# Decayed attention on one core: two maps and 128 tokens to a unit of work, worked out one unit ahead

## The chip, the cores and the metric

The kernel runs on one core of one Trainium2 chip. The metric is the device time of one execution in microseconds (us). Of three runs the median is 2448.79, the lowest 2448.25 and the highest 2448.97.

## What is computed

A model of two blocks on 512 tokens of width 1024, all in fp32. The first block has four sublayers twice over (mixers, cross attention, MLP). The second has three attention branches in a row, each with its own input products, its own gate over the width of the model and its own product back to it; the three are summed and go through one last product. The change touches the attention of the third branch alone, the one with decay ("forgetting attention"): 8 heads of 64, each with a causal map of 512 by 512.

```python
def forgetting_attention(q, k, v, logf):      # q, k, v: 512 tokens x 8 heads x 64
    c = jnp.cumsum(logf, axis=1)
    ...
        s = jnp.einsum('bqhd,bkhd->bhqk', qblk, k).astype(jnp.float32) * scale
        decay = jnp.transpose(cblk, (0, 2, 1))[:, :, :, None] - c_k[:, :, None, :]
        s = jnp.where((dist >= 0)[None, None], s + decay, -jnp.inf)
        p = jax.nn.softmax(s, axis=-1)
        return jnp.einsum('bhqk,bkhd->bqhd', p.astype(v.dtype), v)
...
uc = jnp.einsum('bse,ed->bsd', yc * jax.nn.silu(gc), w_up_c[l])
gates = jax.nn.sigmoid(gm.reshape(B, S, N_BRANCH, D))
merged = gates[:, :, 0] * ua + gates[:, :, 1] * ub + gates[:, :, 2] * uc
```

## The kernel before

All matrices of weights are streamed: SyncE loads panels of 1 MB into `raw` (two slots), ScalarE (ACT) rounds each half of a panel to `w_hi` (L1294), VectorE (DVE) takes the rest as `w_lo` (L2087), and TensorE (PE) forms each product as three: hi by hi, hi by lo, lo by hi (`product3`, L588 to L590). One such triple with 512 columns is called a gate step below, where it belongs to the gates.

The third branch, "c", comes last. Its input products give `QK` (queries of two heads in one tile of 128 partitions: head 2j on partitions 0 to 63, head 2j+1 on 64 to 127; the keys likewise), `BV` (values) and `BG` (the silu of its gate). Then follows the stage that the change is about, `units("c", ...)`. In it PE has two kinds of work in one queue: the attention itself, in plain fp32, and 64 gate steps (`gate_products`), the product for the gate over the width of the model. These are spread over the units by `gate_steps`: 8 ahead of the first unit, the other 56 in even parts.

A unit is one head and one tile t of 128 tokens, 32 in all, t running from 0 to 3 within a head. The keys of tile t are (t + 1) x 128. The steps of a unit:
1. PE, `scores_c` (L1227): one product over 64 partitions, up to 512 columns.
2. DVE, `maxima`: adds the decay of the keys and of the rows on the way out of PSUM (L2752), the mask on the last 128 keys (L2756), and takes the maximum (L2757).
3. ACT, `exps` (L1975): exp in place, with the sum of each row.
4. PE, `turns_c` (L720 by the helper `turn`): t + 1 transposes into one bank; ACT copies them to `PT` (L2022).
5. PE, `values_c` (L1240): t + 1 products into 64 columns; DVE scales by the reciprocal sum (L2776) and by `BG` into `YT` (L2793).

Each fp32 product and each of its weight loads has two records in the trace; a transpose has one. Once a head, ahead of the turns of its t = 1, PE spreads the summed decay of the next head over all partitions (`key_sums`, four transposes by L720), and DVE brings it negated to SBUF (L2810).

The order on each engine is written out by hand. With `AHEAD` 2 the scores of the first two units come first; then for each unit: PE waits for its exp, turns it, issues the scores of the unit after next, then gate steps, waits for the copy, and forms the values. DVE: the reciprocal of the unit, the maxima of the unit after next, at times one split (L2087), the values, at times the key sums. ACT: the copy of the turns, the exps of the unit after next, at times the evacuation of a gate chunk (L2002) and a split (L1294).

PSUM has four banks for the gate products and four "aux" banks for the rest. The aux banks go round: `aux_plan` lists every use in the order of PE's instructions, use n gets bank n mod 4, and PE waits until use n - 4 has been read (`next_aux`). The same list tells DVE and ACT what to wait for.

The first branch, "a", has the same build with two maps to a unit (two maps share a head there), so 16 units, and works one unit ahead: PE issues the scores of the next unit (L1149, two products on the two halves of the partitions), some gate steps, turns (L720), gate steps, values (L1162). DVE forms the weighted difference of both maps (L2770) between exp and turns; PE waits for that. It has 12 gate steps for four units (the third branch: 14 for eight). The second branch works on pairs two units ahead.

Behind the units of "c" come four turns of `YT` (`turned_output`), the product back to the width of the model, and the last product `w_o` with the final norm.

Of the kernel before, what the change touches and what calls it, by code (L numbers as in the profile page):

```python
# [7 lines left out]
ALU = mybir.AluOpType  # L8
# [124 lines left out]
AHEAD = dict(a=1, b=2, c=2)  # L133

def aux_plan():

    e = [("x", k) for k in range(KC)] + [("par", i) for i in range(4)] + [("dt_rows",), ("dt",)]
    e += [("mem", j) for j in range(4)]

    def tile(c):  # L140
        return [("bc", c, q) for q in range(4)] + [("cb", c), ("xs", c, 0), ("xs", c, 1), ("bt", c)]

    e += [("acs",)] + tile(0)
    for c in range(TT):
# [41 lines left out]
    e += [("fc_rows",), ("fc",), ("cc",), ("cb_c", 0)]  # L186
    e += units("C", [(hd, t) for hd in range(8) for t in range(TT)], 1, 1, True) + [("Ct", j) for j in range(4)]
    return e
# [10 lines left out]
         + [("C", (hd, t)) for hd in range(8) for t in range(TT)])  # L199
# [40 lines left out]
def build(nc, w, out):  # L240

    with ExitStack() as ctx:
# [157 lines left out]
        def unit_row(b, u):  # L400
            return (EX[:, 0, 0, :], EX[:, 1, 0, :], EX[:, 0, 1, :] if b == "b" else NC)[unit_slot(b, u)]
# [162 lines left out]
        def _(pe):  # L564
# [539 lines left out]
            def units(b, us, scores, turns, values, before=lambda u: None):  # L1104
# [47 lines left out]
            def turns_a(u, dst):  # L1152
# [30 lines left out]
            def turns_b(u, dst):  # L1183
# [40 lines left out]
            def scores_c(u):  # L1224
                hd, t = u
                a = 64 * (hd % 2)
                pe.matmul(next_aux("C", "S", u, 0)[:, 0:(t + 1) * P], QK[a:a + 64, hd // 2, t * P:(t + 1) * P],  # L1227
                          QK[a:a + 64, 4 + hd // 2, 0:(t + 1) * P], start=True, stop=True).then_inc(aux_done, 1)

            def turns_c(u, dst):  # L1230
                row = unit_row("c", u)
                for kt in range(u[1] + 1):
                    ins = turn(dst[:, kt * P:(kt + 1) * P], row[:, kt * P:(kt + 1) * P])
                return ins

            def values_c(u, dst):
                hd, t = u
                e = UNIT[("C", u)] % 2
                for kt in range(t + 1):
                    ins = pe.matmul(dst[:, 0:64], PT[:, e, kt * P:(kt + 1) * P], BV[:, kt, hd * 64:(hd + 1) * 64],  # L1240
                                    start=(kt == 0), stop=(kt == t))
# [9 lines left out]
            def next_key_sums(u):  # L1251
                if u[1] == 1 and u[0] + 1 < 8:
                    key_sums(u[0] + 1)
# [3 lines left out]
            units("c", [(hd, t) for hd in range(8) for t in range(TT)], scores_c, turns_c, values_c, next_key_sums)  # L1257
# [7 lines left out]
        def _(act):  # L1265
# [653 lines left out]
            for n_, b in enumerate("abc"):  # L1919
# [35 lines left out]
                us = [(hd, t) for hd in range(8 if b == "c" else 4) for t in range(TT)]  # L1955
                B = b.upper()

                def exps(u):
# [3 lines left out]
                    if b == "a":  # L1962
# [3 lines left out]
                    elif b == "b":  # L1966
# [6 lines left out]
                    else:  # L1973
                        v = unit_row(b, u)[:, 0:(t + 1) * P]
                        ins = act.activation(v, v, ACT.Exp, bias=mxs[:, e, 0:1], accum_out=rs[:, e, 0:1])  # L1975
# [35 lines left out]
                for n, u in enumerate(us):  # L2011
# [4 lines left out]
                    if b == "b":  # L2016
# [5 lines left out]
                    free_aux(act.activation(dst, src, ACT.Copy), (B, "T", u, 0))  # L2022
# [46 lines left out]
        def _(dve):  # L2069
# [629 lines left out]
            for n_, b in enumerate("abc"):  # L2699
# [24 lines left out]
                def maxima(u):  # L2724
# [24 lines left out]
                    else:  # L2749
                        row = unit_row(b, u)  # L2750
                        bank = wait_aux(dve, ("C", "S", u, 0))
                        free_aux(dve.scalar_tensor_tensor(row[:, 0:n], EX[:, hd % 2, 1, 0:n],  # L2752
                                                          sm[:, 4 + t, hd:hd + 1], bank[:, 0:n], ALU.add, ALU.add),
                                 ("C", "S", u, 0))
                        aux_read(dve, "C", "S", u, 0)
                        step(dve.tensor_tensor(row[:, n - P:n], row[:, n - P:n], R[:, 0:P], ALU.add))  # L2756
                        ins = dve.tensor_reduce(mxs[:, e, 0:1], row[:, 0:n], AX.X, ALU.max, negate=True)  # L2757
                    ins.then_inc(S["unit_max"], 1)

                def weights(u):  # L2760
# [14 lines left out]
                    else:  # L2775
                        step(dve.reciprocal(rs[:, e, 2:3], rs[:, e, 0:1]))  # L2776

                def values(u, last):
# [12 lines left out]
                    else:  # L2791
                        s = slice(64 * hd, 64 * hd + 64)
                        ins = dve.scalar_tensor_tensor(YT[:, t, s], bank[:, 0:64], rs[:, e, 2:3], BG[:, t, s],  # L2793
                                                       ALU.mult, ALU.mult)
# [13 lines left out]
                def key_sums(hd):  # L2808
                    bank = wait_aux(dve, ("cb_c", hd))
                    free_aux(dve.tensor_scalar(EX[:, hd % 2, 1, :], bank[:, :], -1.0, None, ALU.mult), ("cb_c", hd))  # L2810
                    aux_read(dve, "cb_c", hd)

                us = [(hd, t) for hd in range(8 if b == "c" else 4) for t in range(TT)]
                split_chunks(2 * FIRST_PANEL[f"gm_{b}"] + W_SLOTS)
                if b == "c":
                    key_sums(0)
                for u in us[:AHEAD[b]]:
                    maxima(u)
                for n, u in enumerate(us):
                    weights(u)  # L2820
                    if n + AHEAD[b] < len(us):
                        maxima(us[n + AHEAD[b]])
                    if n:
# [4 lines left out]
                    if b == "c" and u[1] == 1 and u[0] + 1 < 8:  # L2828
                        key_sums(u[0] + 1)
# [86 lines left out]
```

## Time and profile before

The profiled execution took 2449.24 us; its span from first to last instruction is 2447.5 us.

| engine | busy us | share of the span |
|---|---|---|
| PE (matmul) | 2315.3 | 95% |
| DVE | 1304.6 | 53% |
| ACT | 921.1 | 38% |
| POOL | 154.9 | 6% |

The mean granted TensorE clock is 0.973 of full speed. The chain that ended last lies on PE for 83% of the span, on DVE for 10%, on ACT for 5%. How to read it: PE's products are pipelined, the durations of neighbours overlap, so the time that an instruction costs is the distance to the start of the next one. In the timeline equal neighbours are merged: "x8" are eight records, the second number is from the start of the first to the end of the last. A bracket at the end of a line is idle time of that engine ahead of it, and what ended it.

### The profile page before, as it was taken

The page shows a single profiled execution, that of the slowest core. Times are in us where ns is not written, and L with a number is a line of the kernel's source. Part 1 is how long each engine was busy: PE and PEld are TensorE (multiplying, and loading weights), DVE is VectorE, ACT ScalarE, POOL GpSimd, SP SyncE. Part 2 cuts the span into 40 slices and gives each one's busy share as a digit, 9 for nine tenths or more (in the row PEclk, how much of TensorE's full clock was granted, in tenths as well). Part 3 has the DMA queues.
Part 4 walks back from the last instruction along what each step waited for, and adds up shares of the span by engine and source line. Part 5 has one row for each costly group of instructions (what it writes and reads, how often), then busy time and mean ns, then how long its engine had stood idle before and what let it go on. Part 6 is the DMA issues. An engine that isn't in the chain of part 4 may idle for free.

```text
span 2447.5 us, 28890 instructions
## 1 busy us (share of the span) xinstructions
PE 2315.3 (95%) x11792; PEld 1915.0 (78%) x11792; DVE 1304.6 (53%) x1914; ACT 921.1 (38%) x1664; POOL 154.9 (6%) x115
## 2 busy tenths in 40 slices
PE   7999887998999999999899999999989899999998
PEld 6888676876888888888787678888869688779677
DVE  4998678644833334735554383343442833632564
ACT  3353662433423323334433232332333534623343
POOL 0000000040400000400004040000000000000000
PEclk9999889999999999999899999999989999999999
DMA  5332224332333232321142123332322132222112
GB/s 160 87 99 74 89 88 147 134 111 85 98 121 103 86 103 96 111 78 52 53 163 86 52 82 110 103 95 94 103 99 91 35 86 71 68 86 86 35 35 112
DMA packets 187193, 224.75 MB, mean 92 GB/s; under 512 B 16603, under 2 KB 153510, under 8 KB 186038
## 3 DMA queue, kind: packets, MB, share of 16 engines
q1 hardware_dynamic: 174800, 191.90, 24.9%
q10 hardware_dynamic: 11686, 22.62, 2.7%
q0 software_dynamic: 576, 8.39, 0.9%
q8 instruction: 94, 1.54, 0.3%
q14 instruction: 37, 0.30, 0.0%
HBM read 213.72 MB, written 9.18 MB: 91 GB/s over the span
## 4 chain that ended last, share of the span: by engine, by line
PE 83%; DVE 10%; ACT 5%; issue 2%; ACTq 1%; DVEq 0%
PE gemm L588 25%; PE gemm L589 24%; PE gemm L590 24%; PE aux L720 2%; DVE w_lo L2087 2%; PE aux L974 1%; PE aux L955 1%; PE aux L1227 1%; DVE x_lo L2110 1%; DVE work L2225 1%; ACT w_hi L1294 1%; DVE y_plain L2293 1%; PE aux L1240 1%; ACT work L1596 1%; PE aux L1197 0%
## 5 line engine op out<-in xcount | busy, mean ns | idle before, releaser
L2087 DVE TENSOR_TENSOR w_lo<-raw,w_hi 128x1024 fp32r<-128x1024 f32 x250 | 318.4, 1301 | 399.4 <-ACT w_hi L1294 398.7
L588 PE MATMUL gemm<-x_hi,w_hi 128*128 128x512 f32 x1288 | 517.0, 401 | 5.6 <-DVE w_lo L2087 3.2
L589 PE MATMUL gemm<-x_lo,w_hi 128*128 128x512 f32 x1288 | 505.1, 392 | 0.0
L590 PE MATMUL gemm<-x_hi,w_lo 128*128 128x512 f32 x1288 | 504.6, 392 | 0.0
L1294 ACT ACTIVATE w_hi<-raw 128x1024 fp32r<-128x1024 f32 x250 | 254.5, 1052 | 228.1 <-PE gemm L590 225.1
L588 PE MATMUL gemm<-w_hi,x_hi 128*128 128x256 f32 (+2 forms) x992 | 314.1, 317 | 5.7 <-DVE h L2174 5.4
L589 PE MATMUL gemm<-w_lo,x_hi 128*128 128x256 f32 (+2 forms) x992 | 309.4, 312 | 0.0
L590 PE MATMUL gemm<-w_hi,x_lo 128*128 128x256 f32 (+2 forms) x992 | 309.2, 312 | 0.0
L588 PEld LDWEIGHTS gemm<-x_hi,w_hi 128*128 128x128 f32 x1288 | 243.8, 189 | 81.5 <-issue 23.3
L590 PEld LDWEIGHTS gemm<-x_hi,w_lo 128*128 128x128 f32 x1288 | 243.7, 189 | 52.2
L588 PE MATMUL gemm<-w_hi,y_hi 128*128 128x512 f32 (+1 forms) x704 | 270.6, 384 | 10.6 <-DVE y_lo L2159 10.6
L589 PEld LDWEIGHTS gemm<-x_lo,w_hi 128*128 128x128 f32 x1288 | 243.8, 189 | 46.3
L589 PE MATMUL gemm<-w_lo,y_hi 128*128 128x512 f32 (+1 forms) x704 | 268.8, 382 | 0.0
L590 PE MATMUL gemm<-w_hi,y_lo 128*128 128x512 f32 x640 | 250.5, 391 | 0.0
L2083 DVE TENSOR_TENSOR w_lo<-raw,w_hi 128x1024 fp32r<-128x1024 f32 x112 | 134.7, 1221 | 160.0 <-ACT w_hi L1292 151.5
L588 PEld LDWEIGHTS gemm<-w_hi,x_hi 128*128 128x128 f32 x992 | 190.6, 192 | 22.0 <-DVE w_lo L2083 5.8
L589 PEld LDWEIGHTS gemm<-w_lo,x_hi 128*128 128x128 f32 x992 | 190.6, 192 | 10.9 <-issue 0.5
L590 PEld LDWEIGHTS gemm<-w_hi,x_lo 128*128 128x128 f32 x992 | 190.4, 192 | 10.2
L1292 ACT ACTIVATE w_hi<-raw 128x1024 fp32r<-128x1024 f32 x112 | 115.6, 1055 | 214.2 <-PE gemm L590 207.3
L588 PEld LDWEIGHTS gemm<-w_hi,y_hi 128*128 128x128 f32 x704 | 133.6, 190 | 38.2 <-issue 10.3
L589 PEld LDWEIGHTS gemm<-w_lo,y_hi 128*128 128x128 f32 x704 | 133.5, 190 | 25.8 <-issue 0.7
L2293 DVE SCALAR_TENSOR_TENSOR y_plain<-work,par,y_plain 128x512 f32<-128x512 f32 x217 | 149.1, 748 | 4.3 <-ACT y_plain L1498 3.9
(326 smaller groups left out, 2812.2 us busy)
## 6 DMA issues: line engine op xcount, KB each, us to landing
raw<-in_mlp_w_dram SPq DMA_DIRECT2D x64, 1024.0 KB, 5.4
raw<-in_w_in_dram SPq DMA_DIRECT2D x31, 1024.0 KB, 5.3
raw<-in_odd_w_in_dram SPq DMA_DIRECT2D x12, 1024.0 KB, 5.3
raw<-in_even_w_in_dram SPq DMA_DIRECT2D x10, 1024.0 KB, 5.3
raw<-in_even_w_in_dram SPq DMA_DIRECT2D x16, 512.0 KB, 5.5
raw<-in_xa_w_k_dram SPq DMA_DIRECT2D x8, 1024.0 KB, 5.4
raw<-in_xa_w_v_dram SPq DMA_DIRECT2D x8, 1024.0 KB, 5.2
raw<-in_even_w_out_dram SPq DMA_DIRECT2D x8, 1024.0 KB, 5.0
```

The lines of the kernel that those rows point to most:

```text
L588: pe.matmul(dst, a_hi, b_hi, start=first, stop=False)
L589: pe.matmul(dst, a_hi, b_lo, start=False, stop=False)
L590: return pe.matmul(dst, a_lo, b_hi, start=False, stop=last)
L720: return pe.transpose(dst, src, ident[0:src.shape[0], 0:src.shape[0]])
L955: ins = pe.matmul(dst[:, hh * MEM:(hh + 1) * MEM], XQ[:, k, t * P:(t + 1) * P], KT[:, k, :], start=(d == 0), stop=(d == 1))
L974: ins = pe.matmul(dst[:, :], VM[:, m, j * P:(j + 1) * P], PTX[:, m, j // 2, :], start=(m == 0), stop=(m == 1))
L1227: pe.matmul(next_aux("C", "S", u, 0)[:, 0:(t + 1) * P], QK[a:a + 64, hd // 2, t * P:(t + 1) * P], QK[a:a + 64, 4 + hd // 2, 0:(t + 1) * P] ...
L1292: act.activation(piece(w_hi, s), raw_piece(n, s % 2), ACT.Copy).then_inc(w_hi_ready, 1)
L1294: act.activation(w_hi[:, s % W_SLOTS, :, :], raw[:, n % RAW_SLOTS, :, (s % 2) * P:(s % 2 + 1) * P], ACT.Copy).then_inc(w_hi_ready, 1)
L2083: dve.tensor_tensor(piece(w_lo, s), raw_piece(s // 2, s % 2), piece(w_hi, s).bitcast(F32), ALU.subtract).then_inc(w_lo_ready, 1)
L2087: dve.tensor_tensor(w_lo[:, s % W_SLOTS, :, :], raw[:, s // 2 % RAW_SLOTS, :, half], w_hi[:, s % W_SLOTS, :, :].bitcast(F32), ALU.subtract)\
L2293: ins = dve.scalar_tensor_tensor(U[:, f, CONV_W - 1:] if last else acc, U[:, f, i:i + T], par_col("even_conv_w", i * KC + f), acc, ALU.mul ...
```

## The change

Two heads and one tile of 128 tokens make a unit of the third branch: 16 units (pair, t). Their scores are two products, one on each half of the partitions, into two aux banks; the turns go to two banks and are copied by two instructions; the values of both go to one bank. `EX` holds both maps of two units, as in the first branch; the key sums of four heads lie in `y_plain` (the memory of `y_lo`), and the copies of the turns of every second unit lie there too (`pair_weights`). The branch works one unit ahead instead of two. PE issues the scores of the next unit, half of the unit's gate steps, waits for exp, turns both maps, the other half, and the values. DVE takes the maxima of the next unit ahead of the reciprocals of this one. The key sums of heads 0 and 1 come first; those of the next pair come behind the values of t = 0 and t = 1.

```diff
-AHEAD = dict(a=1, b=2, c=2)
+AHEAD = dict(a=1, b=2, c=1)
@@ aux_plan
-            if name == "C" and u[1] == 1 and u[0] + 1 < 8:
-                out += [("cb_c", u[0] + 1)]
...
+            if name == "C" and u[1] < 2 and u[0] + 1 < 4:
+                out += [("cb_c", 2 * u[0] + 2 + u[1])]
...
-    e += units("C", [(hd, t) for hd in range(8) for t in range(TT)], 1, 1, True) + [("Ct", j) for j in range(4)]
+    e += units("C", [(pr, t) for pr in range(4) for t in range(TT)], 2, 2, True) + [("Ct", j) for j in range(4)]
@@ places
+        KEY_SUMS = y_plain[:, 2048:4096].rearrange("p (a b) -> p a b", b=T)
+
+        def pair_weights(u, g):
+            return PT[:, g, :] if UNIT[("C", u)] % 2 == 0 else y_plain[:, T * g:T * g + T]
@@ tensor, units
                 for n, u in enumerate(us):
-                    before(u)
-                    if b == "a":
+                    if b != "b":
                         if n + 1 < len(us):
                             scores(us[n + 1])
                         gate_products(b, (gate_steps(b, n - 1, len(us)) + gate_steps(b, n, len(us))) // 2)
+                    if b == "a":
                         pe.wait_ge(S["p_ready"], UNIT[(name, u)] + 1)
                     else:
                         pe.wait_ge(S["unit_exp"], UNIT[(name, u)] - 2 * TT + 1)
-                    turns(u, next_aux(name, "T", u, 0)).then_inc(aux_done, 1)
-                    if b != "a" and n + 2 < len(us):
+                    for g in range(2 if b == "c" else 1):
+                        turns(u, next_aux(name, "T", u, g), g).then_inc(aux_done, 1)
+                    if b == "b" and n + 2 < len(us):
                         scores(us[n + 2])
                     gate_products(b, gate_steps(b, n, len(us)))
-                    aux_read(pe, name, "T", u, 0)
+                    for g in range(2 if b == "c" else 1):
+                        aux_read(pe, name, "T", u, g)
                     values(u, next_aux(name, "PV", u)).then_inc(aux_done, 1)
+                    after(u)
@@ tensor, scores_c and values_c
+                pr, t = u
+                for g in range(2):
+                    a = 64 * g
+                    pe.matmul(next_aux("C", "S", u, g)[:, 0:(t + 1) * P], QK[a:a + 64, pr, t * P:(t + 1) * P],
+                              QK[a:a + 64, 4 + pr, 0:(t + 1) * P], start=True, stop=True).then_inc(aux_done, 1)
...
+                for g in range(2):
+                    s = slice((2 * pr + g) * 64, (2 * pr + g) * 64 + 64)
+                    for kt in range(t + 1):
+                        ins = pe.matmul(dst[:, 64 * g:64 * g + 64], pair_weights(u, g)[:, kt * P:(kt + 1) * P],
+                                        BV[:, kt, s], start=(kt == 0), stop=(kt == t))
...
             key_sums(0)
-            units("c", [(hd, t) for hd in range(8) for t in range(TT)], scores_c, turns_c, values_c, next_key_sums)
+            key_sums(1)
+            units("c", [(pr, t) for pr in range(4) for t in range(TT)], scores_c, turns_c, values_c, next_key_sums)
@@ scalar
+                    if b == "c":
+                        free_aux(act.activation(pair_weights(u, 0)[:, 0:(u[1] + 1) * P], bank[:, 0:(u[1] + 1) * P],
+                                                ACT.Copy), (B, "T", u, 0))
+                        bank = wait_aux(act, (B, "T", u, 1))
+                        src, dst = bank[:, 0:(u[1] + 1) * P], pair_weights(u, 1)[:, 0:(u[1] + 1) * P]
@@ vector, maxima
+                        for g in range(2):
+                            bank = wait_aux(dve, ("C", "S", u, g))
+                            free_aux(dve.scalar_tensor_tensor(EX[:, e, g, 0:n], KEY_SUMS[:, 2 * (hd % 2) + g, 0:n],
+                                                              sm[:, 4 + t, 2 * hd + g:2 * hd + g + 1], bank[:, 0:n],
+                                                              ALU.add, ALU.add), ("C", "S", u, g))
...
+                        step(dve.tensor_tensor(last, last, over(R[:, 0:P], 2), ALU.add))
+                        ins = dve.tensor_reduce(mxs[:, e, 0:2], EX[:, e, :, 0:n], AX.X, ALU.max, negate=True)
@@ vector, the loop over units
-                    weights(u)
+                    if b != "c":
+                        weights(u)
                     if n + AHEAD[b] < len(us):
                         maxima(us[n + AHEAD[b]])
+                    if b == "c":
+                        weights(u)
```

## Rows read from the trace of the kernel before

**Rows 1.** Busy time of each engine in the stage of the third branch
```profile
core 0: us, PE busy (x) PEld busy (x) DVE busy (x) ACT busy (x) POOL busy (x), PEclk, DMA share, GB/s
...
2253.00:2375.00 122.00, 111.63 (x549) 81.21 (x549) 70.14 (x182) 47.25 (x118) 0.00 (x0) 0.96 0.11 35
```

**Rows 2.** Waits of PE in that stage: us in total, times, longest
```profile
PE aux L720 <- DVE work L2810: 9.3, 7, 2.0
```

**Rows 3.** PE in order of time, one head of the stage (start, us, what)
```profile
2304.30 0.70 PE L1227 MATMUL aux<-work 64*128 64x256 f32 x2
2304.92 0.50 PE L588 MATMUL gemm<-x_hi,w_hi 128*128 128x512 f32 x1
...
2306.41 1.00 PE L1240 MATMUL aux<-work 128*128 128x64 f32 x8
2307.25 0.28 PE L720 MATMUL aux<-ident,work 128*128 128x128 f32 x1
2307.46 0.91 PE L1227 MATMUL aux<-work 64*128 64x384 f32 x2
2308.30 0.50 PE L588 MATMUL gemm<-x_hi,w_hi 128*128 128x512 f32 x1
2309.10 0.33 PE L1240 MATMUL aux<-work 128*128 128x64 f32 x2
2309.27 0.60 PE L720 MATMUL aux<-ident,sm 128*128 128x128 f32 x4
...
2310.02 1.12 PE L1227 MATMUL aux<-work 64*128 64x512 f32 x2
2311.07 0.50 PE L588 MATMUL gemm<-x_hi,w_hi 128*128 128x512 f32 x1
...
2312.57 0.56 PE L1240 MATMUL aux<-work 128*128 128x64 f32 x4
2314.19 0.52 PE L720 MATMUL aux<-ident,work 128*128 128x128 f32 x3 [1.07 <-DVE work L2810]
2314.64 0.49 PE L1227 MATMUL aux<-work 64*128 64x128 f32 x2
2315.05 0.50 PE L588 MATMUL gemm<-x_hi,w_hi 128*128 128x512 f32 x1
...
2316.55 0.78 PE L1240 MATMUL aux<-work 128*128 128x64 f32 x6
2317.16 0.61 PE L720 MATMUL aux<-ident,work 128*128 128x128 f32 x4
2317.70 0.70 PE L1227 MATMUL aux<-work 64*128 64x256 f32 x2
```

**Rows 4.** PE in order of time, a pair of scores in the first branch
```profile
1933.72 1.13 PE L1149 MATMUL aux<-work 64*128 64x512 f32 x4
...
1934.78 0.50 PE L588 MATMUL gemm<-x_hi,w_hi 128*128 128x512 f32 x1
```

**Rows 5.** Groups of equal shape in the third branch's stage: busy us, mean ns
```profile
L2793 DVE SCALAR_TENSOR_TENSOR work<-aux,rs,work 128x64 f32<-128x64 f32 x32 | 9.0, 281 | 17.2 <-PE aux L1240 16.6
...
L2752 DVE SCALAR_TENSOR_TENSOR work<-work,sm,aux 128x512 f32<-128x512 f32 x8 | 6.0, 747 | 6.9 <-PE aux L1227 6.9
...
L2022 ACT ACTIVATE work<-aux 128x512 f32<-128x512 f32 x8 | 4.8, 594 | 8.2 <-PE aux L720 8.2
```

**Rows 6.** DVE and ACT in order of time, a pair in the first branch
```profile
1937.05 1.22 DVE L2734 TENSOR_REDUCE mxs<-work 128x2 f32<-128x1024 f32 x1
...
1939.64 0.19 ACT L1965 ACTIVATION_READ_ACCUMULATOR work<-work,mxs 128x1 f32 x1
```

**Rows 7.** Windows of 4 us, PE alone; the third number group is the granted clock
```profile
2254.00:2258.00 4.00, 4.00 (x12) 0.50 0.18 25
...
2286.00:2290.00 4.00, 4.00 (x19) 0.70 0.80 259
2290.00:2294.00 4.00, 4.00 (x21) 0.88 0.00 0
```

**Rows 8.** Waits of PE in the units of the first branch
```profile
PE aux L720 <- DVE work L2770: 6.2, 6, 1.9
```

More of the change, by code:

```diff
@@ L198 @@
          + [("B", (hd, t)) for hd in range(4) for t in range(TT)]
-         + [("C", (hd, t)) for hd in range(8) for t in range(TT)])
+         + [("C", (pr, t)) for pr in range(4) for t in range(TT)])
 UNIT = {key: n for n, key in enumerate(UNITS)}
@@ L1102, in gate_products, with units @@
                     at["gate"] += 1
-            def units(b, us, scores, turns, values, before=lambda u: None):
+            def units(b, us, scores, turns, values, after=lambda u: None):
                 name = b.upper()
@@ L1224, in scores_c, with turns_c @@
             def scores_c(u):
[L1225 to L1231, printed above, removed]
+                pr, t = u
[3 more added lines that the diff above has]
+                              QK[a:a + 64, 4 + pr, 0:(t + 1) * P], start=True, stop=True).then_inc(aux_done, 1)
+            def turns_c(u, dst, g):
+                e = unit_slot("c", u)
                 for kt in range(u[1] + 1):
-                    ins = turn(dst[:, kt * P:(kt + 1) * P], row[:, kt * P:(kt + 1) * P])
+                    ins = turn(dst[:, kt * P:(kt + 1) * P], EX[:, e, g, kt * P:(kt + 1) * P])
                 return ins
             def values_c(u, dst):
[L1237 to L1241, printed above, removed]
+                pr, t = u
+                for g in range(2):
[3 more added lines that the diff above has]
+                                        BV[:, kt, s], start=(kt == 0), stop=(kt == t))
                 return ins
@@ L1251, in next_key_sums @@
             def next_key_sums(u):
-                if u[1] == 1 and u[0] + 1 < 8:
-                    key_sums(u[0] + 1)
+                if u[1] < 2 and u[0] + 1 < 4:
+                    key_sums(2 * u[0] + 2 + u[1])
             aux_read(pe, "cc")
             key_sums(0)
-            units("c", [(hd, t) for hd in range(8) for t in range(TT)], scores_c, turns_c, values_c, next_key_sums)
+            key_sums(1)
+            units("c", [(pr, t) for pr in range(4) for t in range(TT)], scores_c, turns_c, values_c, next_key_sums)
             turned_output("Ct", "c", 2)
@@ L1954, in _ @@
                 logs()
-                us = [(hd, t) for hd in range(8 if b == "c" else 4) for t in range(TT)]
+                us = [(hd, t) for hd in range(4) for t in range(TT)]
                 B = b.upper()
@@ L1961, in exps @@
                     act.wait_ge(S["unit_max"], UNIT[(B, u)] + 1)
[L1962 removed]
+                    if b != "b":
                         for m in range(2):
@@ L2021, in _ @@
                         src, dst = bank[:, 0:(u[1] + 1) * P], PT[:, e, 0:(u[1] + 1) * P]
-                    free_aux(act.activation(dst, src, ACT.Copy), (B, "T", u, 0))
+                    free_aux(act.activation(dst, src, ACT.Copy), (B, "T", u, 1 if b == "c" else 0))
                     if n + AHEAD[b] < len(us):
@@ L2749, in maxima @@
                     else:
[L2750 to L2754, printed above, removed]
+                        for g in range(2):
[3 more added lines that the diff above has]
+                                                              ALU.add, ALU.add), ("C", "S", u, g))
                         aux_read(dve, "C", "S", u, 0)
-                        step(dve.tensor_tensor(row[:, n - P:n], row[:, n - P:n], R[:, 0:P], ALU.add))
-                        ins = dve.tensor_reduce(mxs[:, e, 0:1], row[:, 0:n], AX.X, ALU.max, negate=True)
+                        aux_read(dve, "C", "S", u, 1)
+                        last = EX[:, e, :, n - P:n]
+                        step(dve.tensor_tensor(last, last, over(R[:, 0:P], 2), ALU.add))
+                        ins = dve.tensor_reduce(mxs[:, e, 0:2], EX[:, e, :, 0:n], AX.X, ALU.max, negate=True)
                     ins.then_inc(S["unit_max"], 1)
@@ L2775, in weights @@
                     else:
-                        step(dve.reciprocal(rs[:, e, 2:3], rs[:, e, 0:1]))
+                        step(dve.reciprocal(rs[:, e, 2:4], rs[:, e, 0:2]))
                 def values(u, last):
@@ L2791, in values @@
                     else:
-                        s = slice(64 * hd, 64 * hd + 64)
-                        ins = dve.scalar_tensor_tensor(YT[:, t, s], bank[:, 0:64], rs[:, e, 2:3], BG[:, t, s],
-                                                       ALU.mult, ALU.mult)
+                        for g in range(2):
+                            s = slice(128 * hd + 64 * g, 128 * hd + 64 * g + 64)
+                            ins = dve.scalar_tensor_tensor(YT[:, t, s], bank[:, 64 * g:64 * g + 64],
+                                                           rs[:, e, 2 + g:3 + g], BG[:, t, s], ALU.mult, ALU.mult)
                     free_aux(ins, (B, "PV", u))
@@ L2809, in key_sums @@
                     bank = wait_aux(dve, ("cb_c", hd))
-                    free_aux(dve.tensor_scalar(EX[:, hd % 2, 1, :], bank[:, :], -1.0, None, ALU.mult), ("cb_c", hd))
+                    free_aux(dve.tensor_scalar(KEY_SUMS[:, hd % 4, :], bank[:, :], -1.0, None, ALU.mult), ("cb_c", hd))
                     aux_read(dve, "cb_c", hd)
-                us = [(hd, t) for hd in range(8 if b == "c" else 4) for t in range(TT)]
+                us = [(hd, t) for hd in range(4) for t in range(TT)]
                 split_chunks(2 * FIRST_PANEL[f"gm_{b}"] + W_SLOTS)
@@ L2816, in _ @@
                     key_sums(0)
+                    key_sums(1)
                 for u in us[:AHEAD[b]]:
@@ L2827, in _ @@
                         gated(n - 1)
-                    if b == "c" and u[1] == 1 and u[0] + 1 < 8:
-                        key_sums(u[0] + 1)
+                    if b == "c" and u[1] < 2 and u[0] + 1 < 4:
+                        key_sums(2 * u[0] + 2 + u[1])
                 split_chunks(2 * FIRST_PANEL[f"gm_{b}"] + W_SLOTS + KC - 1)
```

15 lines of the change are left out of this document (6 added, 9 removed).

## The prediction

> **What bounds the kernel now.** I read the page first, then the busy time by stretches, then the waits of PE inside the stretch, and at last the instructions of that stretch in order of time. The stage of decayed attention is one stretch of 122 us, and PE is busy in 111.63 of it, DVE in 70.14, ACT in 47.25 [rows 1]. So PE carries it, and what can be won is of two kinds: PE's own instructions, and the holes in which it waits. The only large hole has one name: the turns of a unit (L720) wait for DVE's key sums (L2810), 9.3 us in 7 waits [rows 2]. Why: the aux banks are dealt out in turn, four of them, and the turns of unit t = 2 get the bank that the key sums of the next map took four places earlier; DVE empties that bank only after it has worked off the scores of unit t = 3.
>
> One map of a steady stretch shows all of it [rows 3]. Read the distances between starts, since the durations overlap. From the scores of t = 1 at 2304.30 to the same place one map later at 2317.70 are 13.40 us, two maps 26.80. In it:
> - scores: 0.62 (t = 1), 0.84, 1.05, 0.41, together 2.92; the length goes with the keys
> - a gate step (three products of 512 columns): 0.80 alone right behind scores (2308.30 to 2309.10), 1.49 for two (2304.92 to 2306.41): 0.69 each, and 0.11 once after scores
> - values: 0.84 for eight records (t = 3), 0.17 for two (t = 0), 0.61 for six, so 0.39 for four: 2.01 a map, 0.11 a record
> - key sums and the turns of t = 1: 0.75 for six transposes; the turns of t = 0, 2, 3 are 0.21, 0.45, 0.54. This is 0.11 for each transpose and 0.10 more before scores. Key sums are then 0.44
> - the wait: 1.62 from the values of t = 1 to the turns of t = 2, of which 0.39 are values: 1.23.
>
> **The change part by part.**
> Scores. Two maps of one unit are now issued one after the other on rows 0 to 63 and 64 to 127. The first branch does just this already, and there the pair of t = 3 takes from 1933.72 to 1934.78, 1.06 us [rows 4], where one map alone takes 1.05 [rows 3]. So a pair costs what one did: bounds are 1.06 (side by side) and 2.10 (one behind the other), and I take the lower, since it is the same shape, type and array half. Per two maps that removes 2.92 us.
> The 0.10 ahead of scores and the 0.11 behind them appear at every group of scores; of eight per two maps four go: 0.4 + 0.44 removed.
> The Trainium skill, "TensorEngine Tiling (Array Packing)", section "Key Properties", says that changing the tiling mode drains TensorE; the trace agrees in kind, by the 0.10 and 0.11 just read.
>
> Turns and values. The number of transposes and of products stays. Of the turns, 20 per two maps at 0.11 are 2.2, now behind gate steps and ahead of gate steps, so without the switch to half the array. Values: a pair is twice one, plus 0.05 as the records run on without a break: 4.22 per two maps.
> Key sums. Two per two maps, 0.88, now placed behind the values of t = 0 and t = 1.
> Gate steps: 56 over 16 units, 3.5 each, in the order 1 and 2 (t = 0, 2), 2 and 2 (t = 1, 3): ahead of the turns and behind them. Fourteen per two maps, 9.66.
> The new sum per two maps: 9.66 + 4 x 0.11 + 2.92 + 4 x 0.10 + 2.2 + 4.22 + 0.88 = 20.7 us, if PE never waits.
>
> The waits. The key-sum wait goes: key sums now take the bank that the second turns of the next unit get, and DVE empties it ahead of the maxima of the unit after next, with a pair of scores and the first gate steps in between. What is late next? With one unit ahead, the turns of t = 3 need exp of t = 3, whose scores were issued one unit earlier. From the end of the scores PE has: one gate step 0.80, turns of t = 2 0.66, two gate steps 1.38, values 1.27, the switch 0.10, scores of the next t = 0 0.41, two gate steps 1.49: 6.1 us. DVE and ACT need in that time: two sums at 0.75 [rows 5], the mask on 256 elements (not in this trace; between nothing and the 0.75 of 512 elements, I take 0.4), the maximum over 1024 elements 1.22, which ends at 1938.27, and the exp pair with its sums until 1939.83, 1.56 [rows 6]: 4.7. Slack 1.4. At the very last unit no scores follow, so 0.6 less: 0.8. Shorter t have less to do in the chain and about the same gate steps above it.
> ACT now has two copies behind the turns, 0.59 each [rows 5], and PE's values wait for the second. Two gate steps, 1.38, stand between; the first copy starts while the second map still turns (0.44), so the copies end some 0.8 us after the turns: hidden, slack 0.6. Behind the copies queue the exps of the next unit and the gate evacuation; they have the slack above. If this cover were gone, each unit would pay up to 0.8 us, 13 in all.
> On DVE the reciprocal now stands behind the maxima of the next unit and ahead of the split and the values. The turns do not use it, only the values do on their way out, so nothing on PE waits. DVE's work stays near 70 us, of a stage that would be some 97 long. Other edits cost nothing: the same bytes at other places (the low half of y is free in this stage, the last readers of it being the products ahead of it), and one more key sum before the first scores, counted below. No DMA is added; SP's loads of the next weights wait for DVE's splits, which go by PE's gate steps, so they move with PE.
>
> **The sum.** 26.8 - 20.7 = 6.1 per two maps, four times 24.4. Added: the waits were in truth 7, and longer at the first maps; 9.3 us plus 7 x 0.16 for the rest of each hole are 10.4, where eight times 1.23 are 9.8: 0.6 more. In the windows from 2286 to 2294 the granted clock fell to 0.70 and 0.88, behind a second long wait; 4 x 0.30 + 4 x 0.12 = 1.7 us lost there [rows 7], and with the waits gone I expect this back. Taken off: the second key sum at the stage's start, where the clock is at 0.50 (1.2 of 2.4 GHz) [rows 7], 0.9 of which I count 0.6; one more 0.28 [rows 5] of DVE before the last turns, and 0.2 for small holes. Result 24.4 + 0.6 + 1.7 - 0.6 - 0.3 - 0.2 = 25.6 us. The profiled execution took 2449.24 (span 2447.5), so 2423.6; it stands 0.45 above the median of the runs, so 2423.2.
>
> **The rivals.**
> First: the chain from scores over DVE and ACT to the turns comes bare, since one unit ahead is less than two. For it speaks the first branch, which works one ahead on pairs and waits 6.2 us in 6 waits for DVE [rows 8]. Against it: there DVE's weighted difference of both maps stands between exp and turns, and the maxima of the next unit stand behind that, so each lateness is handed on; here neither holds, and there are 14 gate steps where the first branch has 12. Its price is that of the first branch: 6.2, giving 2429.4.
> The Trainium skill, "TensorEngine Tiling (Array Packing)", section "PSUM Bottleneck", warns that tiling speeds up TensorE but not PSUM evacuation, and names this same outcome; the first branch's waits are what this trace has of it.
> Second: the pair does not run side by side in this stage. Then the scores cost 2.92 more per two maps: 11.7, giving 2434.9. What the first branch shows speaks against it [rows 4].
> Third, slower than before: the chain is bare in full. If ACT reaches the exps of a unit only when PE already stands at its turns, each unit pays the whole chain behind its scores, 4.7 at t = 3 and about half of that at t = 0, some 3.5 in the mean: 16 x 3.5 = 56 us lost against 25.6 won, giving 2479. It decides from 1.6 us of waiting per unit; with the slack of 1.4 it takes 3 us more in the chain than the rows give. ACT's queue is the place for it (copies, exps, gate evacuation and split in one line), and ACT is busy only 47.25 of 122 [rows 1].
> That the granted clock stays or falls low elsewhere costs about what it did, 1.7, and lies in the forecast's own range.
>
> **How the numbers follow.** Forecast 0.80, its own range 2421 to 2427 (0.6 to either side for the holes, 1.7 if the clock does not come back, up to 2 for copies that are not quite hidden). First rival 0.09, second 0.03, third 0.04, and 0.04 for a mixture that cancels the gain. The range 2420.5 to 2430.5 takes in the forecast and the first rival. What a measurement here can tell from no change is about 0.2%, 4.9 us; the forecast, the first and the second rival are all beyond it. Faster 0.93, same 0.03, slower 0.04.
>
> **What would show it.** The pair of scores of t = 3 at 1.05 to 1.1 us to the next gate product, in 16 groups; no wait of L720 for the key sums; a period of 20.7 us per two maps; the stage some 26 us shorter, and all behind it unchanged and that much earlier; a clock of 1.00 between the stage's start and its end. Wrong would be: waits of the turns for ACT's exp over 1 us per unit, values waiting for the second copy, or a period above 23.

## The result: 27 to 29 us faster, and what the changed kernel's profile shows

The changed kernel takes 2419.33 us (median of 4 runs, 2417.22 to 2421.02) where the kernel before took 2448.52 in the same comparison (2446.81 to 2448.97): a ratio of 0.9882 with a 95% interval from 0.9865 to 0.9899, 29.2 us. Later comparisons, on three chips, gave 0.9890 (0.9875 to 0.9905), 0.9888 (0.9873 to 0.9903) and 0.9888 (0.9871 to 0.9904). All 16 times of the changed kernel together have the median 2418.9 and reach from 2414.3 to 2421.0; 25 times of the kernel before have 2446.8, from 2443.2 to 2449.3. That is 27.9 us between the medians and 27.7 between the means. The forecast was 25.6 us and 2423.2; the time lies 1.2 us below the low end of the stated range, 2420.5.

The profiled execution of the changed kernel took 2417.22 us; its span is 2415.5. First the busy time of its third branch's stage, to be held against [rows 1] (same columns). Lines have moved: L588 to L590 are L594 to L596 now, L720 is L726, L1227 is L1237, L1240 is L1251, L2810 is L2827.

```profile
2247.00:2341.00 94.00, 93.02 (x540) 74.08 (x540) 60.50 (x131) 43.14 (x114) 0.00 (x0) 0.96 0.14 45
```

PE is busy in 93.02 of 94 us; it had holes of 10 us in [rows 1]. The waits of PE from 2250 to 2350 are these two and no others. The key sums' 9.3 us of [rows 2] are gone and nothing has come in their place:

```profile
PE aux L726 <- DVEq L2815: 0.7, 1, 0.7
PE gemm L594 <- DVE y_lo L2124: 0.3, 1, 0.3
```

Now one pair of heads in order of time, the counterpart of [rows 3] (start, us, what). It begins and ends at the scores of t = 1:

```profile
2278.53 0.70 PE L1237 MATMUL aux<-work 64*128 64x256 f32 x4
2279.16 0.50 PE L594 MATMUL gemm<-x_hi,w_hi 128*128 128x512 f32 x1
...
2279.96 0.38 PE L726 MATMUL aux<-ident,work 128*128 128x128 f32 x2
2280.10 0.48 PE L594 MATMUL gemm<-x_hi,w_hi 128*128 128x512 f32 x1
...
2281.57 0.55 PE L1251 MATMUL aux<-work 128*128 128x64 f32 x4
2281.96 0.60 PE L726 MATMUL aux<-ident,sm 128*128 128x128 f32 x4
2282.49 0.92 PE L1237 MATMUL aux<-work 64*128 64x384 f32 x4
2283.34 0.50 PE L594 MATMUL gemm<-x_hi,w_hi 128*128 128x512 f32 x1
...
2288.02 1.13 PE L1237 MATMUL aux<-work 64*128 64x512 f32 x4
2289.08 0.50 PE L594 MATMUL gemm<-x_hi,w_hi 128*128 128x512 f32 x1
...
2295.20 1.03 PE L726 MATMUL aux<-ident,work 128*128 128x128 f32 x8
2295.99 0.47 PE L594 MATMUL gemm<-x_hi,w_hi 128*128 128x512 f32 x1
...
2297.46 1.89 PE L1251 MATMUL aux<-work,y_plain 128*128 128x64 f32 x16
2299.28 0.70 PE L1237 MATMUL aux<-work 64*128 64x256 f32 x4
```

The scores are four records now, and yet as short as two were: 1.06 us at t = 3 (2288.02 to 2289.08), 0.85 at t = 2, 0.63 at t = 1, against 1.05, 0.84 and 0.62 for one map in [rows 3]. The period is 2299.28 - 2278.53 = 20.75 us; 20.7 was worked out, and 26.80 it was.

How near does the chain from scores over DVE and ACT come to the turns? This is the unit of t = 3 across the engines, from its scores to its turns:

```profile
2267.26 1.13 PE L1237 MATMUL aux<-work 64*128 64x512 f32 x4
2268.49 1.41 DVE L2766 SCALAR_TENSOR_TENSOR work<-y_plain,sm,aux 128x512 f32<-128x512 f32 x2 [0.43 <-PE aux L1237]
2270.00 0.42 DVE L2772 TENSOR_TENSOR work<-work 128x256 f32<-128x256 f32 x1
2270.46 1.22 DVE L2773 TENSOR_REDUCE mxs<-work 128x2 f32<-128x1024 f32 x1
2271.72 0.72 ACT L1977 ACTIVATE work<-work,mxs 128x512 f32<-128x512 f32 x1 [1.19 <-DVE mxs L2773]
...
2273.05 0.19 ACT L1977 ACTIVATION_READ_ACCUMULATOR work<-work,mxs 128x1 f32 x1
...
2274.45 1.04 PE L726 MATMUL aux<-ident,work 128*128 128x128 f32 x8
```

The scores are done at 2268.3, exp at 2273.24, the turns start at 2274.45: a chain of 4.9 us (4.7 forecast) and a slack of 1.2 (1.4 forecast). The mask on 256 elements, which no row of before showed, takes 0.42; the forecast took 0.4.

### The profile page after: what moved, and what is told of

The parts are those of the page before. It is cut to its first block, busy times and chain, and to the rows that moved or that the text cites. A ratio compares the mean times of both kernels' runs of the same rounds, so it can differ in the third digit from the quotient of the medians.

```text
span 2415.5 us, 28810 instructions
## 1 busy us (share of the span) xinstructions
PE 2293.1 (95%) x11792; PEld 1904.8 (79%) x11792; DVE 1296.4 (54%) x1866; ACT 919.0 (38%) x1664; POOL 155.0 (6%) x115
## 4 chain that ended last, share of the span: by engine, by line
PE 83%; DVE 10%; ACT 5%; issue 2%; ACTq 1%; DVEq 0%
PE gemm L594 25%; PE gemm L595 24%; PE gemm L596 24%; PE aux L726 2%; DVE w_lo L2101 2%; PE aux L980 1%; PE aux L961 1%; DVE x_lo L2124 1%; ACT w_hi L1306 1%; DVE work L2239 1%; PE aux L1251 1%; DVE y_plain L2307 1%; ACT work L1608 1%; PE aux L1237 1%; PE aux L1206 0%
## 5 line engine op out<-in xcount | busy, mean ns | idle before, releaser
L594 PE MATMUL gemm<-x_hi,w_hi 128*128 128x512 f32 x1288 | 515.8, 400 | 6.1 <-DVE w_lo L2101 3.7
L596 PE MATMUL gemm<-x_hi,w_lo 128*128 128x512 f32 x1288 | 504.2, 391 | 0.0
L594 PE MATMUL gemm<-w_hi,x_hi 128*128 128x256 f32 (+2 forms) x992 | 313.8, 316 | 5.7 <-DVE h L2188 5.4
L596 PE MATMUL gemm<-w_hi,x_lo 128*128 128x256 f32 (+2 forms) x992 | 309.1, 312 | 0.0
L594 PEld LDWEIGHTS gemm<-x_hi,w_hi 128*128 128x128 f32 x1288 | 243.4, 189 | 75.0 <-issue 17.1
L596 PEld LDWEIGHTS gemm<-x_hi,w_lo 128*128 128x128 f32 x1288 | 243.0, 189 | 51.9
L594 PE MATMUL gemm<-w_hi,y_hi 128*128 128x512 f32 (+1 forms) x704 | 271.5, 386 | 10.6 <-DVE y_lo L2173 10.6
L596 PE MATMUL gemm<-w_hi,y_lo 128*128 128x512 f32 x640 | 250.5, 391 | 0.0
L594 PEld LDWEIGHTS gemm<-w_hi,x_hi 128*128 128x128 f32 x992 | 190.2, 192 | 22.0 <-DVE w_lo L2097 5.8
L596 PEld LDWEIGHTS gemm<-w_hi,x_lo 128*128 128x128 f32 x992 | 190.1, 192 | 10.3
L594 PEld LDWEIGHTS gemm<-w_hi,y_hi 128*128 128x128 f32 x704 | 134.4, 191 | 38.2 <-issue 10.3
```

The lines of the kernel that those rows point to most:

```text
L594: pe.matmul(dst, a_hi, b_hi, start=first, stop=False)
L596: return pe.matmul(dst, a_lo, b_hi, start=False, stop=last)
```

## Where the other microseconds come from: the same code, executed again

From the first key sums (2248.00) to the last turns (2340.16) the stage takes 92.2 us. Before it took 118.7 (2253.49 to 2372.18). So the stage gave 26.5. But the profiled executions differ by 32.0 us (2449.24 and 2417.22), and the rest, 5.5 us, was already there when the stage began. These are the first instructions of the third branch's sums of decay, in code that is the same in both, in the two first profiles (the kernel before, the changed kernel):

```profile
2250.80 0.39 PE L1220 MATMUL aux<-sm,triu 128*128 128x8 f32 x2 [0.69 <-ACT work L1952]
```

```profile
2245.02 0.39 PE L1229 MATMUL aux<-sm,triu 128*128 128x8 f32 x2 [0.69 <-ACT work L1964]
```

5.8 us apart, ahead of every changed instruction. The same windows of both, PE alone (busy, granted clock, DMA), show what differs: the granted clock. First the kernel before, then the changed one.

```profile
200.00:360.00 160.00, 139.13 (x892) 0.89 0.26 88
...
1180.00:1370.00 190.00, 170.47 (x785) 0.92 0.27 92
```

```profile
200.00:360.00 160.00, 139.41 (x911) 0.91 0.26 88
...
1180.00:1370.00 190.00, 170.57 (x780) 0.93 0.27 92
```

0.02 of 160 us and 0.01 of 190 are 5 us. Is that the change, or chance? Two runs repeat the two kernels without an edit.

> The kernel before, unchanged, profiled once more. Question: the first profiles of before and after differ by 5.6 us in code that is the same in both, ahead of the third branch's units, at places where one of them shows a granted clock of about 0.5 for some 3 us and the other does not. If that is chance from execution to execution, this profile has its low-clock stretches at other places than the first of before, and the time up to the first key sums of the third branch moves by 1 to 5 us. If it belongs to the kernel, the stretches lie where they lay and that time agrees within 0.5 us. The stage itself, from the first key sums to the last turns: 118.7 us again, or 1.7 less if its second dip of the clock is absent.

Measured: one time, 2449.09 us, where seven plain runs of the same kernel on that chip had 2443.18 to 2448.28. The profile puts the sums of decay at 2250.61, the clock at 0.89 and 0.92 in the two windows, the stage at 118.7 with the same dip. It is a twin of the first profile, so this run alone speaks for the rival.

> The changed kernel, unchanged, timed again. Stage theory: the change is worth its stage, 26.3 us by the first pair of profiles (25.6 were forecast), and the rest of the measured 29.2 is chance of the clock elsewhere; then the difference here lies between 24 and 29 and the stage is 92.6 us again within 0.5. Rival: the change also helps the code ahead of it (another layout of the program); then this profile too is some 5 us ahead of both of before when the third branch's stage begins, and the difference is 29 or more.

Measured: 2419.13 us (2417.68 to 2420.45), where before had 2445.96: 26.8 us. The sums of decay stand at 2245.47, the stage takes 92.2. The difference is within the 24 to 29 of the stage theory; the profile is again 5 us early, as the rival had it.

The clock records of all the profiles tell what the 5 us are made of, but not what decides them. Added up from the start to the first sums of decay, the time at half clock is 119.5 us in both profiles of the kernel before; 109.2 in three and 112.6 in one of the four of the changed kernel; 105.8 in the kernel of the next section, which is the kernel before with one small edit in the third branch (its sums of decay stand at 2244.59, earlier than any); and 116.1, 116.1 and 102.4 in the next three kernels, which are small edits of the changed one. Half of such time is lost. Take that half from the place of the sums of decay, and 2190.4 to 2191.7 is left in ten of the thirteen profiles (2192.3 to 2194.8 in the other three). So nearly all of the 5 us is time at half clock, in code that is the same. It does not go with the change as such, since a small edit of either kernel moves it by 3 to 7 us. That it is pure chance is not shown either: the profiles of one and the same kernel agree within 0.2 us (before) and 1.9 us (changed) at the sums of decay. What the plain times show is that 5 us are not gained for good: the profiled executions of the kernel before, 2449.24 and 2449.09 us, lie above 24 of its 25 plain times. What makes an execution take more or less of its time at half clock there was not found.

## Experiments on the parts

**The key sums' bank.** The kernel before, single maps, two ahead, with nothing changed but the place of the key sums:

```diff
@@ aux_plan, units
-            if name == "C" and u[1] == 1 and u[0] + 1 < 8:
-                out += [("cb_c", u[0] + 1)]
             turns = [(name, "T", u, j) for j in range(nt)]
...
             if pv:
                 out += [(name, "PV", u)]
+            if name == "C" and u[1] == 1 and u[0] + 1 < 8:
+                out += [("cb_c", u[0] + 1)]
@@ tensor, units
                 for n, u in enumerate(us):
-                    before(u)
...
                     values(u, next_aux(name, "PV", u)).then_inc(aux_done, 1)
+                    before(u)
```

> The kernel before with one part of the change: the key sums of the next head are issued behind the values of t = 1 and not ahead of its turns, so they get another aux bank. Single maps, two ahead, as before. Bank theory: the wait of the turns of t = 2 for DVE's key sums goes, 7 x 1.49 = 10.4 us, and the second dip of the clock with it, 1.7: 2436.5 to 2438.5. Rival (DVE's order, not the bank, is what they wait for): the wait only changes its name, and the time stays within 3 us of before.

Measured: 2434.78 us (2431.78 to 2438.00) against 2445.96, ratio 0.9954 (0.9938 to 0.9971), 11.2 us; the stage takes 107.2 instead of 118.7, 11.5 us less. The theory had 12.1 us in all. The four times stand in two pairs 6 us apart (2431.78 and 2432.04, 2437.53 and 2438.00), so the stage is the firmer number. One head's key sums and what follows, to be held against the 1.62 us hole in [rows 3]:

```profile
2299.66 0.55 PE L1240 MATMUL aux<-work 128*128 128x64 f32 x4
2300.05 0.60 PE L720 MATMUL aux<-ident,sm 128*128 128x128 f32 x4
2300.49 0.49 PE L720 MATMUL aux<-ident,work 128*128 128x128 f32 x3
2300.91 0.49 PE L1227 MATMUL aux<-work 64*128 64x128 f32 x2
```

The turns of t = 2 follow the key sums at once. DVE's order is as it was, so it was the bank and not DVE's order that held PE. In the stage the clock stays at 1.00 from 2260 to 2357, once its start is over: the dip of [rows 7] from 2286 on is gone with the holes. So 11.5 of the 26.5 us, two fifths of the stage's gain, need no pairs at all.

**The pair side by side.** The changed kernel with one gate step between the two scores:

```diff
-                        if n + 1 < len(us):
+                        if n + 1 < len(us) and b == "c":
+                            scores(us[n + 1], 0)
+                            gate_products(b, gate_steps(b, n - 1, len(us)) + 1)
+                            scores(us[n + 1], 1)
+                        elif n + 1 < len(us):
                             scores(us[n + 1])
```

> The changed kernel with one gate step put between the two scores of a pair, so that they cannot run side by side; the number of instructions stays. If the pair runs side by side in the changed kernel, this costs the second score in full, 2.92 us per two maps or 11.7, and for each of 15 pairs once more the switch ahead of it and behind it, 0.21 or 3.2: 15 us slower than the changed kernel. If the pair there ran one behind the other, only the 3 us of switches come on top.

Measured: 2433.97 us (2433.32 to 2434.34), 14.8 above the changed kernel on the same chip. The stage takes 104.9, 12.7 more, though the clock at its start was better: 0.79 and 0.78 in the windows of 4 us from 2250 on, 1.7 us lost, where the changed kernel had 0.50 and 0.65, 3.4 us. The pair of t = 3 there:

```profile
2296.70 1.12 PE L1241 MATMUL aux<-work 64*128 64x512 f32 x2
2297.75 0.50 PE L594 MATMUL gemm<-x_hi,w_hi 128*128 128x512 f32 x1
...
2298.64 1.12 PE L1241 MATMUL aux<-work 64*128 64x512 f32 x2
2299.70 0.87 PE L726 MATMUL aux<-ident,work 128*128 128x128 f32 x6
```

The two scores take 1.05 us and 1.06 us here; together they take 1.06 us in the changed kernel. This is the second score at full price, and the forecast's second rival falls. The Trainium skill, "TensorEngine Tiling (Array Packing)", section "Key Properties", says that different tiles can run their products in parallel and that a change of the tiling mode drains TensorE. The trace agrees with the first by the 1.06 us for both scores. It agrees with the second in kind: the gate step between the scores takes 0.89 us from 2297.75 to 2298.64, where a step amid others takes 0.69. Without its clock, which was 1.7 us better, this stage is 14.4 us longer than that of the changed kernel; that is what the pairs are worth, for 15 of the 16. The two parts, 11.5 of the stage by the bank and 14.4 by the pair, make 25.9 of the 26.5.

**The slack of one unit ahead.** The changed kernel with k idle copies on ACT (128x512 onto itself) between the maximum and exp of every unit:

```diff
                     act.wait_ge(S["unit_max"], UNIT[(B, u)] + 1)
+                    if b == "c":
+                        for _ in range(k):
+                            step(act.activation(NC, NC, ACT.Copy))
```

> The changed kernel with one more ACT instruction (a copy of 128x512 onto itself, with a wait for its end) in every unit of the third branch, between the maximum and exp: some 0.7 us longer chain from scores to turns, 16 times. If the chain has the slack that was worked out (1.4 us at t = 3, 0.8 at the last unit, more at the others), this costs nothing: the changed kernel's time within 1 us, and PE waits nowhere. If the chain is bare, as the first rival had it, it costs 16 x 0.7 = 11 us.

> The same with three such copies, some 2.1 us more in each unit's chain. Slack of 1.4 us at t = 3: exposed by 0.7 there and by 1.3 at the last unit, and the two copies behind the turns are late where a gate chunk is evacuated ahead of them; in all 3 to 8 us more than the changed kernel, with waits of the turns for ACT's exp at t = 3 first. No slack: 34 us.

Measured for one copy (0.67 us from its start to exp's): 2420.20 us (2419.83 to 2421.39), 1.3 above the changed kernel's 2418.9; PE waits for ACT at no turns. The 1.3 is less than single runs of one kernel spread, and whether it is a cost or chance stays open; the 11 us of a bare chain are not there. The stage of this profile takes 91.1 us with 1.7 lost to half clock, where the changed kernel has 92.2 with 3.4: 0.6 more without the clock. For three copies: 2424.71 us (2422.90 to 2426.99), 5.8 above; the stage takes 96.9, 4.7 more, and the only wait of PE for another engine in its units is the one foretold, of the turns for exp. It is shown twice, at the products and at the weight loads ahead of them (PEld):

```profile
PE aux L726 <- ACT work L1980: 3.0, 4, 1.1
```

```profile
PEld aux L726 <- ACT work L1980: 5.2, 5, 1.5
```

The second is nearer to what it costs, since a product's record runs on into the wait. One unit of t = 3, from the last gate product to the turns:

```profile
2297.11 0.40 PE L596 MATMUL gemm<-x_hi,w_lo 128*128 128x512 f32 x1
...
2297.93 0.19 ACT L1980 ACTIVATION_READ_ACCUMULATOR work<-work,mxs 128x1 f32 x1
...
2298.17 1.09 PE L726 MATMUL aux<-ident,work 128*128 128x128 f32 x8 [0.67 <-ACT work L1980]
```

The turns start 1.06 us after the last gate product, where in the changed kernel they start 0.23 after it (2274.22 to 2274.45). So 2.0 us more in the chain expose 0.83 us here, and about 1.2 was slack; the last unit, which the forecast had 0.6 tighter, waits longest (1.1 us at the products). The 5.2 us of the weight loads carry the stage's 4.7. The chain is covered, and the first and third rival fall.

**Beyond the change.** Two waits of PE were left at the edges of the stages: 0.69 us for ACT's last evacuation at the start of each branch's attention, and 0.7 us for DVE before the last turns. Gate steps can stand over both:

```diff
             gemm("g_c", x_hi, x_lo)
+            gate_products("c", 3)
             chunk_read(pe, stage_end_chunk("g_c") - 1)
...
-    return KC + (KC * KC - (2 if b == "a" else 1) * KC) * (n + 1) // units
+    return KC + (KC * KC - (2 if b == "a" else 1) * KC - (0 if b == "a" else 2)) * (n + 1) // units
```

The kernel "edges" has the first edit in all three branches and the second; "gates_first" has the first in the third branch alone.

> The changed kernel with PE's gate steps also where it still waits: in each branch 3 of the first 8 steps are issued ahead of the wait for ACT's last evacuation (0.69 us of waiting at each of the three, and in the third branch the few small products there are followed by a stretch at half clock), and in the second and third branch 2 of the last steps are held back behind the last values, where PE waits 0.7 us for DVE. Same work in another order. Theory: 3 x 0.7 + 0.7 + 0.3 = 3 us, and 1.7 to 3.4 more if the half clock at the start of the third branch's stage goes: 2413 to 2416 where the changed kernel has 2419. Rival: the waits move to the next step (turns waiting for exp of the first unit) and nothing is won.

> The changed kernel once more, as the yardstick of the other three and for the spread of its times. By the earlier runs: median 2418 to 2420, single runs from 2417 to 2421, the stage 92.2 us, and the low-clock stretches ahead of the stage again at partly other places.

> One edit of the one before it alone: in the third branch 3 of the first 8 gate steps are issued ahead of the wait for ACT's last evacuation. Clock theory: the half clock at the start of that stage follows on the 0.69 us wait and the small products; with gate steps over the wait the stretch is absent, 3.4 us, and 0.7 of wait with it: 4 us in the profile, 2415 in the median. If the median shows less than 2 us, the chip takes the stretch at half clock elsewhere in most executions.

> The reordered gate steps of all three branches again, since its four times ran from 2412.3 to 2420.0 and do not tell. If it is worth its 5 us of the profile, the median is 2413 to 2415 on this chip where the changed kernel has 2418 to 2420; if the clock takes back what the order wins, within 1 us of the changed kernel.

> The changed kernel as the yardstick of the other two on the same chip: 2418 to 2420, the stage 92.2 us.

Measured, in the order of the two comparisons: edges 2418.35 us (2412.27, 2417.93, 2418.78, 2419.99) beside 2418.85 of the changed kernel (2418.28 to 2420.47); then edges 2414.21 (2413.06 to 2414.62) and gates_first 2416.43 (2414.63 to 2418.41) beside 2418.43 (2414.34 to 2420.43). The eight times of edges have the median 2414.5, the changed kernel's sixteen 2418.9; between the means are 3.2 us, with a standard error of 1.1. The first comparison shows nothing, the second 4 us, as the theory had it; together they make a gain of 3 to 4 us likely. Against the kernel before the ratio is 0.9871 (0.9856 to 0.9886) in the second, the lowest of all kernels here. For gates_first the theory had 4 us and 2.0 were measured, which the spread of four times does not tell from nothing. The rival, that a wait only moves on, holds for most of the 0.69 us of the first two branches: in the second the turns wait 1.4 us for ACT instead of 0.7, in the first they wait 6.8 us for DVE instead of 6.3.

In the first profile of edges the half clock at the stage's start is absent: the granted clock is 1.00 where the changed kernel has 0.50 and 0.65 in the first eight microseconds. These are windows of "edges" and then of the changed kernel, PE alone:

```profile
2244.00:2248.00 4.00, 4.00 (x29) 1.00 0.00 0
2248.00:2252.00 4.00, 3.71 (x23) 1.00 0.00 0
2252.00:2256.00 4.00, 4.00 (x20) 1.00 0.86 262
```

```profile
2247.00:2251.00 4.00, 3.72 (x17) 0.50 0.00 0
2251.00:2255.00 4.00, 4.00 (x13) 0.65 0.81 256
```

But the second profile of edges, the same kernel, has it again:

```profile
2248.00:2252.00 4.00, 4.00 (x16) 0.50 0.11 14
2252.00:2256.00 4.00, 4.00 (x15) 0.69 0.75 248
```

In the profile of gates_first it was there in part, 0.77 and 0.81 in the two windows from 2248 on; but so it was in two kernels without this reordering, "apart" and the one with one idle copy (1.7 us lost instead of 3.4 in each). So it is not shown that the gate steps over the wait do anything to the clock. The wait for DVE ahead of the last turns is gone in both profiles of edges.

## Why the prediction fell short

Point by point:
- The bound. Right: PE carried the stage, and the one large hole was the aux bank of the key sums. The kernel with that edit alone shows it.
- The scores. Right: bounds were 1.06 and 2.10, 1.06 was taken and measured; the first branch's pair was the right row.
- The new sum per two maps. Right: 20.7 against 20.75.
- The waits. Right: none came in place of the old one; slack 1.4 forecast, 1.2 read from the profile and about 1.2 from the three copies. The rivals of a bare chain, partly or in full, had no ground. The 6.2 us of the first branch [rows 8], which spoke for them, are waits for DVE's weighted difference, which reads and writes SBUF; they are no case of a PSUM bank emptied late.
- The clock's second dip, 1.7 us. Right; it went with the holes.
- What was taken off, 1.1 us in all, was mis-sized. The second key sum at the stage's start was to cost 0.6, and cost nothing. These are the first key sums, the scores and the first gate product behind them, in the kernel before and in the changed one:

```profile
2253.49 1.12 PE L720 MATMUL aux<-ident,sm 128*128 128x128 f32 x4 [0.28 <-DVE sm L2718]
2254.53 1.65 PE L1227 MATMUL aux<-work 64*128 64x128 f32 x4
2256.11 0.79 PE L588 MATMUL gemm<-x_hi,w_hi 128*128 128x512 f32 x1
```

```profile
2248.00 1.97 PE L726 MATMUL aux<-ident,sm 128*128 128x128 f32 x8 [0.28 <-DVE sm L2732]
2249.90 0.80 PE L1237 MATMUL aux<-work 64*128 64x128 f32 x4
2250.63 0.79 PE L594 MATMUL gemm<-x_hi,w_hi 128*128 128x512 f32 x1
```

Both take the same, 2.62 and 2.63 us, all at half clock. The key sums take 0.86 more. The scores take 0.85 less: before, they are those of t = 0 and t = 1 of one head, one behind the other; now they are the pair of t = 0 alone, and t = 1 comes later, at full clock. I had also counted double: the sum for two maps, taken four times, holds all eight key sums already. The 0.2 for small holes found none, and the last turns cost 0.2 instead of 0.3. With these the sum makes 26.5 for the stage instead of 25.6.
- The step that failed is the one from the stage to the whole time, and so the range. The forecast took 2448.8, the median of three runs within 0.7 us, for a yardstick good to a few tenths, and gave the low end, 2.7 us below the forecast, only what the stage could give, although it put what a measurement can tell at 4.9 us. But the same kernel has taken 2443.2 to 2449.3 since. These times go with the granted clock of the whole execution (0.976 in the fastest, 0.972 in the slowest), so with time at half clock, and the profiles place it in code that was not touched. Half of that spread, 3 us, belonged below the forecast as well as above. Against all times together the miss of 4.3 us (2423.2 to 2418.9) is made of three terms: 2.0 for the yardstick (2448.8, where the median of 25 times is 2446.8), 0.9 for the stage, and 1.4 beyond the stage. Between the means the last is 1.2, with a standard error of 0.6: at the edge of chance, and it can as well be a small effect of the program on the clock ahead, where the changed kernel's profiles had less time at half clock. Which of the two stays open. Of the 29.2 us first measured 26.5 are the stage; the other 2.7 are more than the 0.3 to 0.9 that the later three comparisons left beyond it (26.8, 27.4 and 27.3).

## What to carry to other kernels

Where products over 64 partitions come in twos, put them side by side, on the two halves of the partitions, and in one group: here the second cost 0.01 us (1.06 for 1.05), and each group cost a switch of some 0.2 us (0.10 ahead, 0.11 behind), with one score in it or with two. Where four PSUM banks go round in PE's order, a use that another engine empties late blocks the fourth use behind it; moving it in the order, from ahead of the turns to behind the values, was worth 11 us without any other change. And a range for a small effect has to hold the spread of the untouched code, which three runs do not show.

## What the runs showed of the hardware

The granted clock is not the same from execution to execution in identical code: 0.89 to 0.94 in the same 160 us, and 6 us between whole executions of one kernel. I had expected the differences to be a few tenths, as the first three runs had them. A stretch at half clock (granted 0.50, 1.2 of 2.4 GHz) stood at the start of the third branch's stage in twelve of the thirteen profiles, behind waits of PE and small products, but not always as long: 1.7 or 3.4 us were lost in it. With gate steps put over the wait it was absent in one profile and back in another of the same kernel.
